# Block 2's first projection: tiles 2 and 3 turned between TensorE's blocks

## What is computed

```python
def rmsnorm(x, g):
    xf = x.astype(jnp.float32)
    y = xf * lax.rsqrt(jnp.mean(xf * xf, axis=-1, keepdims=True) + RMS_EPS)
    return (y * g.astype(jnp.float32)).astype(x.dtype)

def second_block(x, ...):
    for l in range(DEPTH_2):
        h = rmsnorm(x, mix_norm_g[l])
        x = x + mixing_layer(h, ...)
        h = rmsnorm(x, ffn_norm_g[l])
        x = x + swiglu(h, w_gate[l], w_up[l], w_down[l])
    return rmsnorm(x, final_norm_g)

def mixing_layer(h, ...):
    u = jnp.einsum("bsd,de->bse", h, w_in)
    a_b, a_c, a_x, q, k, v, c_in = jnp.split(u, offs, axis=-1)
    ...
```

## Time and profile before

| | |
|---|---|
| median of 3 runs | 2708.0 us |
| lowest and highest | 2707.09 and 2708.52 us |
| span of the profiled execution | 2705.5 us (its time is not listed apart from the span) |
| TensorE busy | 2639.9 us, 98% of the span |
| ScalarE, VectorE, GpSimd busy | 832.5, 1005.3 and 801.9 us |
| chain that ended last | 89% TensorE, 4% VectorE, 3% ScalarE |

### The profile page before, as it was taken

How to read it: one execution, slowest core, us unless ns; L and a number is a source line. 1 busy time by engine, 2 the same in 40 slices (tenths; PEclk the granted TensorE clock), 3 DMA queues, 4 the chain that set the end, 5 groups by cost and what they waited for, 6 DMA issues and landing times.

```text
span 2705.5 us, 35632 instructions
## 1 busy us (share of the span) xinstructions
PE 2639.9 (98%) x14540; PEld 1979.1 (73%) x14540; DVE 1005.3 (37%) x1837; ACT 832.5 (31%) x1460; POOL 801.9 (30%) x643
## 2 busy tenths in 40 slices
PE   7999999999999999999999899999999999999998
PEld 4777777886558885544453797988888987988887
DVE  3656566623432153222121696300011786200012
ACT  3444444423433241000000427322223336322222
POOL 2222223320114430000000342344455433444453
PEclk9999999999999999999999899999999999999999
DMA  7122222001104229999999321232222221233221
GB/s 276 53 65 71 77 74 62 31 26 61 46 30 141 94 80 372 426 427 426 426 427 425 121 86 47 79 94 94 95 98 88 94 79 48 78 95 106 96 94 47
DMA packets 189046, 382.41 MB, mean 141 GB/s; under 512 B 11889, under 2 KB 146933, under 8 KB 163317
## 3 DMA queue, kind: packets, MB, share of 16 engines
q1 hardware_dynamic: 187712, 379.59, 37.8%
q10 hardware_dynamic: 1205, 0.99, 0.1%
HBM read 378.46 MB, written 2.10 MB: 141 GB/s over the span
## 4 chain that ended last, share of the span: by engine, by line
PE 89%; DVE 4%; ACT 3%; DMA 1%; issue 1%; SPq 1%; DVEq 1%; POOL 0%; ACTq 0%
PE bank L1684 14%; PE bank L1689 14%; PE bank L1688 14%; PE bank L1974 12%; PE bank L1452 5%; PE bank L1921 2%; PE bank L1486 2%; PE bank L1548 2%; PE bank L1557 1%; PE bank L1738 1%; PE bank L1561 1%; PE bank L1467 1%; DMA place<-in_w_down 1%; PE bank L1755 1%; PE bank L1660 1%
## 5 line engine op out<-in xcount | busy, mean ns | idle before, releaser
L755 POOL TENSOR_TENSOR w_lo<-ring,w_hi 128x512 fp32r<-128x512 f32 x384 | 521.6, 1390 | 671.5 <-ACT w_hi L805 671.5
L805 ACT ACTIVATE w_hi<-ring 128x2048 fp32r<-128x2048 f32 x96 | 184.0, 1917 | 622.9 <-PE bank L1684 622.9
L1684 PE MATMUL bank<-hT_hi,w_hi 128*128 128x512 f32 (+1 forms) x928 | 352.7, 380 | 3.4 <-DVE conv_acc L2913 1.6
L1689 PE MATMUL bank<-hT_hi,w_lo 128*128 128x512 f32 (+1 forms) x928 | 347.8, 375 | 0.0
L1688 PE MATMUL bank<-hT_lo,w_hi 128*128 128x512 f32 (+1 forms) x928 | 347.6, 375 | 0.0
L1684 PEld LDWEIGHTS bank<-hT_hi,w_hi 128*128 128x128 f32 x928 | 174.8, 188 | 35.4 <-DVE hT_lo L2815 2.0
L1689 PEld LDWEIGHTS bank<-hT_hi,w_lo 128*128 128x128 f32 x928 | 174.7, 188 | 31.7
L1688 PEld LDWEIGHTS bank<-hT_lo,w_hi 128*128 128x128 f32 x928 | 174.9, 188 | 30.6 <-issue 1.0
L3006 DVE TENSOR_TENSOR ffn_hT<-ffn_sg,bank 128x512 f32<-128x512 f32 x44 | 30.3, 688 | 414.8 <-PE bank L1689 414.8
L755 POOL TENSOR_TENSOR w_lo_m<-ring,w_hi_m 128x512 fp32r<-128x512 f32 x64 | 82.4, 1320 | 302.3 <-ACT w_hi_m L805 302.3
L1452 PE MATMUL bank<-hT,head_w 128*128 128x512 f32 x336 | 156.9, 593 | 0.0
(11 more groups left out here) (525 smaller groups left out, 5239.7 us busy)
## 6 DMA issues: line engine op xcount, KB each, us to landing
ring<-in_w_gate SPq DMA_DIRECT2D x56, 1024.0 KB, 7.7
ring<-in_w_down SPq DMA_DIRECT2D x52, 1024.0 KB, 7.8
ring<-in_w_up SPq DMA_DIRECT2D x46, 1024.0 KB, 8.6
place<-in_w_up SPq DMA_DIRECT2D x40, 1024.0 KB, 18.3
place<-in_w_down SPq DMA_DIRECT2D x34, 1024.0 KB, 24.9
ring<-in_w_in SPq DMA_DIRECT2D x33, 1024.0 KB, 5.2
place<-in_w_gate SPq DMA_DIRECT2D x30, 1024.0 KB, 23.9
head_w<-in_w_in SPq DMA_DIRECT2D x32, 512.0 KB, 4.9
```

The source lines that it names most:

```text
L755: last = pool.tensor_tensor(w_lo[m % 2][:, cs], src[:, cs], w_hi[m % 2][:, cs].bitcast(F32), ALU.subtract)
L805: return act.activation(dst, src, ACT.Copy)
L1684: first = mm(dst, a[0], b[0], start=start, stop=False)
L1689: return mm(dst, a[1], b[0], start=False, stop=stop)
```

## The change

Only TensorE's program changes. In the first layer tiles 0 and 1 are turned, then block 0 of the early tokens is projected, then tile 2 is turned, then block 1 is projected, then tile 3 is turned. The second layer's order, and that of all other engines, stays.

```diff
-            for t in range(TT):
-                turn_tile(0, t)
+            turn_tile(0, 0)
+            turn_tile(0, 1)
             first_projection(0, 0)
+            turn_tile(0, 2)
             for l in range(LAYERS):
                 m = M_IN
                 first_projection(l, 1)
+                if l == 0:
+                    turn_tile(0, 3)
                 tiles_ready(l * 2, TT)
```

## The result

The changed kernel takes 2716.01 us (median of 9 runs, 2714.87 to 2717.78) beside 2708.52 us for the kernel before (9 runs, 2707.09 to 2710.17): 7.5 us more, a ratio of 1.0028 with a 95% interval of 1.0020 to 1.0036. It is slower, by a little more than the forecast's 6.8 us and within its range.

A forecast was written before the change was run, and what follows sets the result against it. TensorE, 98% busy, was taken as the bound, with its waits at the hand-over to block 2. Wait 3.7 + first slow clock 2.2 + second 1.3 - 0.4 = 6.8 us on 2708.0 gave 2714.8 us, range 2711.2 to 2717.4.

The forecast's parts named there:

- Block 0's start: First layer's early projection: block 0 starts at 1517.92, released by tile 1's low part, after TensorE idles from 1512.73.
- Block 0 at half clock: Behind the 5.2 us gap, block 0's products mostly at 0.24 us spacing; costs 1.6 to 2.9 us, 2.2 taken.
- The turnings and block 1: TensorE pieces behind block 0: tile 2's turning takes 1.7 us and block 1 takes 2.9 us.
- Tile 3's chain: From tile 3's turning to the late half, uncovered: turning, gain, high part, low part take 5.03 us as in layer two.
- The bounds of 4.1 and 5.7: Limits in us for tile 3's chain, with undisturbed or slowest low parts; loss 2.8 or 4.4 us.
- The late half's start: Chunk 0's late half starts at 1530.45 instead of 1526.76, 3.7 us later; block 0's clock loss of 2.2 us comes on top.
- The second fall: Clock falls again in the 3.1 us gap behind tile 3's turning; costs 0 to 1.7 us, 1.3 taken.
- What is taken off for the kernel before: 0.4 us subtracted, since some executions of the kernel before may lose 0.9 us to a late clock ahead of projection.
- Clock spared: Rival: clock returns early after the first gap and does not fall again; only the 3.7 us wait stays, 2711.7; chance 0.20.
- Given back in the attention: Rival: TensorE's waits in block 2's attention absorb 2.8 us, 4.0 us stay, 2712.0; chance 0.07.
- Both gaps at their dearest: Rival: chain 5.7 us, first slow stretch 2.9, second 1.7 and part of another, about 9.5 us: 2717.5; chance 0.08.
- As meant: Rival: block 0 starts 3.0 us earlier at the hand-over to block 2 and the rest follows, 2705.0; chance 0.03.

The follow-up runs named there:

- split_later: The changed kernel with ScalarE's splitting of chunk 1 moved behind tile 3's high part, so GpSimd is silent during tile 3's low parts: 2713.86 us.
- tile3_fill: Against the kernel before: tile 3 alone turned between block 0 and block 1, plus 9 idle products ahead of tile 2's turning: 2708.38 us.
- tile3_between: Half of the change: tile 3 turned between block 0 and block 1, tile 2 kept in front of block 0: 2707.78 us.
- both_between: Against the changed kernel: tile 3's turning also moved ahead of block 1, so tiles 2 and 3 both stand between the blocks: 2715.69 us.
- fill_first: The changed kernel with 20 idle products of 512 columns in the gap ahead of block 0: 2714.78 us.
- before_fill: The kernel before with 9 idle products of 512 columns between the turnings of tiles 1 and 2: 2707.40 us.
- tile3_split: Against the kernel before: tile 3 alone turned between the blocks, and chunk 1's splitting moved behind tile 3's high part, no idle products: 2707.96 us.

## Why the prediction was right

Taken from tile 0's diagonal, so that the two traces can be laid over each other (1.45 us between them):

- **Block 0's start.** Forecast 1517.92 - 1505.70 = 12.22 us behind the diagonal; measured 1519.47 - 1507.15 = 12.32. Released by tile 1's low part, behind 5.48 us of idle time (5.2 forecast).
- **Block 0 at half clock.** Forecast 2.2 us. Measured 1524.09 - 1519.47 = 4.62, 1.7 us over 2.9. The products stood (1523.02 - 1519.82) / 15 = 0.213 us apart until the clock came back at about 1523.3, not the 0.24 that I had named as a sign. At full clock they stand 0.12 us apart, so a product at half clock loses 44% of its time and not 50%. The Trainium skill, "TensorE: Matmul & The Clock Gate", section "Back-to-back issue gap", has N / 1.2 ns for N columns at half clock and N / 2.4 + 2.5 ns at full; worked out for 256 columns that is an estimate of 213 ns, which the trace meets, and one of 109 ns, which the trace's 120 ns exceed. The forecast had 3.7 to 5.9 us of slow work; it was 3.8 (1519.47 to about 1523.3), at the lower end, and my 2.2 was oversized by 0.5.
- **The turnings and block 1.** 1.71 and 2.95 us; forecast 1.7 and 2.9.
- **Tile 3's chain.** Forecast 5.03 us from the second layer; measured 1534.08 - 1528.75 = 5.33. The 0.3 are in the low parts, 2.68 us for the two against 2.38. GpSimd worked over the whole of both pairs, so it is not that it covered more here; it had begun 0.6 us after the turning here and 1.4 us in the second layer, so the low parts fell at another place among its four instructions. Over all traces with GpSimd at work the pair took 2.38 to 3.08 us. How that place sets the length, no run here takes apart. The bounds of 4.1 and 5.7 have both been met: 4.12 in split_later with GpSimd silent, 5.67 in tile3_fill.
- **The late half's start.** 5.9 us later than before (1534.08 - 1507.15 = 26.93 against 21.06). Forecast 3.7 + 2.2 = 5.9: the chain's 0.3 and 0.15 at block 0's start and in the pieces made up for the clock's 0.5. That the sum met this closely is luck, as two terms were missed in opposite directions.
- **The second fall.** Forecast 1.3 us; measured 1541.18 - 1534.08 = 7.10 against 5.80, 1.3.
- **What is taken off for the kernel before.** Forecast 0.4 us, for executions where its clock comes back late. Nothing shows it: the medians are 7.5 us apart where the profiles are 7.17 apart in A, and filling the gap of the kernel before gave the same A. The runs cannot resolve 0.4 us, so this term stays open. A clock that comes back late does occur: tile3_between's trace, whose order is the same up to the turning of tile 2, has it 6 us after that turning began. How often the kernel before has it is not known. The term is what kept the forecast under the result in A (6.8 against 7.17, where 7.2 would have stood without it). The other part of the distance by the medians is the base: the forecast started from 2708.0, the median of 3 runs, and 9 runs gave 2708.52.
- **The rivals.** Clock spared: no, both falls came. Given back in the attention: no, the waits and B are unchanged, and a delay of 6.8 us in A passed through. Both gaps at their dearest: no, 5.33, 1.7 and 1.3 us stand where it had 5.7, 2.9 and over 1.7. As meant: block 0 did start 2.9 us earlier, counted from tile 0's diagonal (12.32 against 1520.96 - 1505.70 = 15.26), and the order still lost, since the turning it was put ahead of had been free.

By A, then, of the 7.2 us about 4.3 are the wait with the turnings behind block 0 (forecast 3.7), and 2.9 the clock (forecast 3.5, less the 0.4). What turns the balance is which tile moves: tile 3 alone, between the blocks, costs nothing that the medians show; with tile 2 moved too, either order costs 7 us.

## What to carry to other kernels

Before work is moved on the busiest engine, ask of each piece whether it now stands in idle time: such a piece is free (tile 2's turning took 3.57 or 2.05 us in the old place, and A was the same), and moved out of it it delays what stands behind it, here with the clock on top. Start a long chain before the work that does not need it, and keep that work behind it as cover: with tile 3 alone between the blocks, its turning and the 2.9 us of block 1 covered all but 0.37 us of a chain of 5.2 us. And measure such edits from a landmark just ahead of the place to one just behind it, since most of the runs' spread of 2 to 5 us comes from elsewhere. What is left in that distance is the clock at the place, which can still move it by a microsecond.

## What the hardware showed that I had not expected

- The granted clock fell to 0.50 at gaps of 2.17 us (split_later), 2.18 (both_between) and 2.4 (before), there after work had resumed, and stayed at 1.00 at gaps of 0.97 (fill_first), 1.96 (before_fill, ahead of tile 3's turning) and 0.85 us (tile3_fill). When it comes back differs from one execution to the next: 3.7 us after work resumed in the trace of before, 3.8 in the changed kernel's, 6 in tile3_between.
- VectorE and GpSimd slow each other: a pair of low parts goes from 1.29 us (1.47 with a short wait for the high part inside) to between 2.38 and 3.08 us, a chunk's splitting from 5.0 to 5.9 us.
- Everything behind chunk 1's first product, 1173 us, is the same to 0.2 us in all twelve traces, while the way to tile 0's diagonal differs by 4 us in kernels that are the same up to there. Most of that goes with the clock, which also falls far ahead of the place, in the first block, while TensorE has no idle time. A stretch from the trace of before (us, busy PE, PEld, DVE, ACT, POOL, granted clock, DMA share, GB/s):

```profile
624.50:628.00 3.50, 3.50 (x19) 3.50 (x18) 0.00 (x0) 0.00 (x0) 0.00 (x0) 0.51 0.96 312
```

  Up to 1498 us TensorE was at half clock for no time in tile3_between (diagonal at 1504.1), for 3.4 us in before (1505.7), for 6.8 us in the changed kernel (1507.15), and for 10.2 us in tile3_split (1508.3). With the 44% lost at half clock, 3.4 us more of it are 1.5 us, which is the whole distance between the two spans ahead of the place. The other traces follow to about 1 us. Just ahead of the fall near 622 in the changed kernel TensorE had gone from products of 512 columns to products of one column; why some executions have the fall and others not stays open.
